# Keys' norm per token and head: root and reciprocal on a 128x10 tile, spread back over the channels by TensorE

## The chip, the cores and the metric

The kernel runs on one core of one Trainium2 chip. The metric is the device time of one launch in microseconds, the lower the better.

## The reference

Two layers of a trunk for 128 prompt tokens and 512 latent tokens (640 together, five tiles of 128). The even layer mixes tokens with a bidirectional RWKV-7 scan over 12 heads of 64 channels. The part that the change touches is the normalised key of each token and head, which enters the scan twice, as `kk` and as `kk * a`:

```python
kf = k.astype(f32)
kk = heads(kf * k_k)
kk = kk / jnp.maximum(jnp.linalg.norm(kk, axis=-1, keepdims=True), 1e-12)
...
s_kk = jnp.einsum('zbhvk,zbhk->zbhv', S, kk_t)
S = (S * w_t[..., None, :] - s_kk[..., None] * (kk_t * a_t)[..., None, :]
     + v_t[..., :, None] * k_t[..., None, :])
```

After the scan come a group norm, a bonus term and a gate, then the output projection, and after each mixer an expert-choice mixture of 16 SwiGLU experts. The odd layer has a convolution and a chunked gating in place of the scan. All arithmetic is in 32-bit floats.

## The kernel before, in words

The twelve heads are handled as six head pairs: a pair's 2 x 64 channels lie on the 128 partitions and its 640 tokens on the free axis. `even_heads` does all six. It first builds the features of pair 0 (called the opening below), then runs `heads(True)` five times and `heads(False)` once. Each engine runs its own queue in the order written, and the engines meet only in named semaphores.

A turn of `heads(True)` scans pair i and, in the gaps that the scan leaves, builds the features of pair i+1. Its first part masks the products of queries and keys (VectorE, L1574) and inverts them (the many 64x64 matmuls L1014 to L1060 and L1582). Its second part is a chain of four steps j = 0 to 3 that passes the state from tile to tile. A step goes through: `old_state(j)` on TensorE (L952, L955), a copy on ScalarE, a matmul (L1103), a copy on ScalarE, a pair of matmuls (L1115, L1116), and `advance(j)` on VectorE (L1600, L1603), which lets `old_state(j+1)` go. Between these links TensorE takes pieces for the next pair from the table `FILL` by `ahead(n)`, with n = 3j, 3j+1 and 3j+2: the projections of queries (Q) and values (VV), chunk by chunk (L893), and `knorm`. Its third part sums the outputs y (L1125 to L1134), multiplies the gate (L1140) and takes the mean over a head (L1144); then the next turn begins with L972.

The norm is made as follows. ScalarE squares the scaled key into `kk`, a 128x640 tile (`k_squares`). `knorm` multiplies it by `headones`, a 128x128 matrix with ones where both channels are of the same head, so that every channel gets its head's sum (L909). ScalarE takes the root of the 128x640 result (`k_root`, L1233), and VectorE in `normed_k` the maximum with 1e-12 (L1435), the reciprocal (L1437) and the product with the key (L1439). `norm_features` (L1469, L1471) and `key_queries` (L1486) read the result.

`shift(s)` (L1422, L1424) blends each token of Q, K or VV with its neighbours. Before it ScalarE copies the projection (`copy_raw`, L1194) and GpSimd adds the neighbours (L1368). `copy_raw(VV)` also waits for `r_shifted`, which `shift(Q)` gives. `bonus_input` (L1476) gives `ahead_done`, on which ScalarE's copy of y waits (L1321); after that copy TensorE can take the mean (L1144).

In the opening, TensorE's order is: projection of K, low ranks, `knorm(2)`, projection of Q, a slab of the modulation weights (`slabs`, L463), projection of VV, three slabs, and `mod_turn` (L474), which waits for ScalarE's `copy_rows`. VectorE's order is: `shift(K)`, both decays, both `key_features` (the last of them L1462 and L1463), `normed_k`, `norm_features`, `shift(Q)`, queries, `shift(VV)`, `bonus_input`, then `take_mods` (L491), which waits for `mod_turn`, and then the masks L1574. Only after `take_mods` may TensorE do its second group of L972 (`ymean_read`).

Of the kernel before, what the change touches and what calls it, by code (L numbers as in the profile page):

```python
# [17 lines left out]
ALU = mybir.AluOpType  # L18
# [7 lines left out]
P = 128  # L26
# [4 lines left out]
NT = T // P  # L31
# [38 lines left out]
def build(nc, t):  # L70
    ctx = ExitStack()
    with ctx:
# [42 lines left out]
        def pair(q):  # L115
            return psf[:, q * 1024:q * 1024 + T]
# [650 lines left out]
        def even_heads():  # L767
# [30 lines left out]
            ecc = ca(2, NT)  # L798
            proj, shf, rkv, kk = x[:, 0:2], x[:, 2:4], x[:, 4:7], x[:, 7]
# [27 lines left out]
            with stage() as block:  # L827
# [54 lines left out]
                def _(pe):  # L882
# [22 lines left out]
                    def knorm(q):  # L905

                        pe.wait_ge(sem("sq_ready"), 1).then_inc(sem("sq_ready"), -1)
                        for a, b in halves:
                            last = pe.matmul(pair(q)[:, a:b], headones, kk[:, a:b], start=True, stop=True)  # L909
                        last.then_inc(sem("e_ready"), 1)  # L910

# [7 lines left out]
                    def take_weights():  # L919
# [9 lines left out]
                        6: (lambda: slot_read(2), lambda: project(VV, 0, (0, 1))),  # L929
# [3 lines left out]
                        10: (lambda: project(VV, 0, (7,)),),  # L933
# [235 lines left out]
                    slot_read()  # L1169
                    project(Q, 0, range(KC))  # L1170
# [4 lines left out]
                    slot_read(3)  # L1175
                    mod_turn(pe, PARTS - EARLY, 5)
# [5 lines left out]
                def _(act):  # L1182
# [47 lines left out]
                    def k_root(q):  # L1230

                        act.wait_ge(sem("e_ready"), 1).then_inc(sem("e_ready"), -1)
                        act.activation(kk, pair(q), ACT.Sqrt).then_inc(act_done, 1)  # L1233
                        done("e_read", "knorm_root")
# [149 lines left out]
                def _(dve):  # L1384
# [47 lines left out]
                    def normed_k():  # L1432

                        dve.wait_ge(sem("knorm_root"), 1).then_inc(sem("knorm_root"), -1)
                        dve.tensor_scalar(kk, kk, 1e-12, None, ALU.max).then_inc(dve_done, 1)  # L1435
                        done()
                        dve.reciprocal(kk, kk).then_inc(dve_done, 1)  # L1437
                        done()
                        dve.scalar_tensor_tensor(kk, rkv[:, K], col("k_k"), kk, ALU.mult, ALU.mult).then_inc(dve_done, 1)  # L1439
                        done()  # L1440

# [125 lines left out]
                    def heads(i, following):  # L1567
# [56 lines left out]
                        if following:  # L1624
                            key_features(1)
                            normed_k()
                        advance(2)
                        if following:
                            norm_features(0)
                            norm_features(1)  # L1630
                            shift(Q)
# [22 lines left out]
                    normed_k()  # L1654
# [1151 lines left out]
```

## Time and profile before

| what | us |
|---|---|
| median of 3 runs (2413.72, 2414.37, 2420.5) | 2414.37 |
| span of the profiled execution | 2406.1 |
| the six reciprocals of 128x640 (L1437), first and last start | 174.5, 753.1 |

The profiled execution has no whole time of its own on record, only its span from first to last instruction; the median of the runs lies 8.3 us above it. TensorE is busy 94% of the span (2250.6 us), VectorE 40%, ScalarE 16%, GpSimd 7%. The even layer's heads fill 152 to about 860 us; most of the remainder are the two expert mixtures, in which the DMA row of the page stands at 9, that is 90% or more. A share of busy time says little here, because within a turn the engines hand work to each other: the views in order of time, engine by engine, are the ones to read.

### The profile page before, as it was taken

How to read it: one execution, taken by the hardware profiler on the slowest of the kernel's cores; microseconds unless marked ns; L12 is line 12 of the kernel's file. 1: busy time of each engine (PE TensorE's matmuls, PEld its weight loads, DVE VectorE, ACT ScalarE, POOL GpSimd, SP SyncE). 2: the span in 40 equal slices, each digit the busy share in tenths (PEclk: the TensorE clock that was granted, in tenths of full speed). 3: DMA queues.
4: the chain of work that ended last, by engine and by line, in shares of the span. 5: the costliest groups of instructions: out<-in, count | busy, mean ns of one | idle time of the engine just before them, and what ended most of it. 6: DMA issues, size and time to landing. Idle time of an engine off the chain costs nothing. (4 is left out here: it accounts for less than half of the span.)

```text
span 2406.1 us, 55266 instructions
## 1 busy us (share of the span) xinstructions
PE 2250.6 (94%) x23172; PEld 1269.3 (53%) x23172; DVE 965.6 (40%) x1785; ACT 396.9 (16%) x685; POOL 166.7 (7%) x162
## 2 busy tenths in 40 slices
PE   5998998989899789999999999889998999999997
PEld 2446776767676665544444444545555444444444
DVE  2357767676777621311111111479613111111113
ACT  2022323232323201100000000211312000000001
POOL 1001010000011000000000000000000000000000
PEclk8998999999999999999999999899999999999999
DMA  9971010101010026699999999602036999999995
GB/s 370 391 308 32 3 33 3 33 3 34 4 33 21 3 69 244 247 379 396 396 392 397 392 395 392 211 1 70 1 140 246 396 397 395 392 397 392 392 391 173
DMA packets 181703, 539.12 MB, mean 224 GB/s; under 512 B 12545, under 2 KB 54145, under 8 KB 181410
## 3 DMA queue, kind: packets, MB, share of 16 engines
q1 hardware_dynamic: 175202, 515.16, 55.6%
q0 software_dynamic: 6336, 21.63, 3.8%
q8 instruction: 119, 1.95, 0.3%
q14 instruction: 46, 0.38, 0.0%
HBM read 510.81 MB, written 25.95 MB: 223 GB/s over the span
## 5 line engine op out<-in xcount | busy, mean ns | idle before, releaser
L2045 PE MATMUL ps<-raw,xs 128*64 128x512 f32 x3072 | 670.9, 594 | 4.2 <-PEq L2039 4.2
L2045 PEld LDWEIGHTS ps<-raw,xs 128*64 128x64 f32 x3072 | 217.3, 137 | 428.6 <-issue 427.2
L2057 PE MATMUL ps<-raw,xs 128*32 128x256 f32 x6144 | 342.5, 380 | 2.3 <-PEq L2039 2.2
L2057 PEld LDWEIGHTS ps<-raw,xs 128*32 128x32 f32 x6144 | 195.2, 110 | 133.2 <-issue 9.9
L2236 DVE SCALAR_TENSOR_TENSOR h<-h,ps 128x768 f32<-128x768 f32 x32 | 30.5, 953 | 461.2 <-DVEq L2235 461.2
L893 PE MATMUL ps<-h,wk 128*128 128x512 f32 (+1 forms) x576 | 175.3, 444 | 1.5 <-PEq L1160 1.3
L1582 DVE COPY_PREDICATED wk<-m,ps 128x512 f32<-128x512 uint8 x180 | 130.7, 732 | 98.7 <-DVEq L1581 97.7
L893 PEld LDWEIGHTS ps<-h,wk 128*128 128x128 f32 x576 | 93.3, 190 | 76.2 <-issue 73.6
L2363 PE MATMUL ps<-h,raw 128*128 128x512 f32 (+1 forms) x448 | 124.7, 440 | 7.2 <-PEq L2354 7.2
L2164 ACT ACTIVATE h<-ps 128x768 f32<-128x768 f32 x32 | 26.0, 811 | 591.8 <-ACTq L2163 591.8
L1020 PE MATMUL ps<-wk 64*64 64x64 f32 x2400 | 107.3, 224 | 10.2 <-issue 7.0
L1026 PE MATMUL ps<-wk 64*64 64x64 f32 x2160 | 100.3, 222 | 3.8 <-issue 3.8
L1039 PE MATMUL ps<-wk 64*64 64x64 f32 x2400 | 99.0, 218 | 4.9 <-issue 4.7
L2363 PEld LDWEIGHTS ps<-h,raw 128*128 128x128 f32 x448 | 69.0, 193 | 62.4 <-issue 62.4
L1277 ACT ACTIVATE wk<-ps 128x256 f32<-128x256 f32 (+1 forms) x180 | 65.7, 366 | 191.2 <-ACTq L1276 191.0
L2624 DVE SCALAR_TENSOR_TENSOR wk<-wk 128x670 f32<-128x670 f32 x116 | 96.3, 905 | 0.4 <-DVEq L2618 0.4
L2020 POOL DMA_INDIRECT ysum<-rows,idx x30 | 43.1, 1438 | 752.4 <-POOLq L2018 743.5
L1020 PEld LDWEIGHTS ps<-wk 64*64 64x64 f32 x2400 | 86.1, 133 | 15.2 <-issue 10.6
L1039 PEld LDWEIGHTS ps<-wk 64*64 64x64 f32 x2400 | 86.7, 135 | 4.9 <-issue 4.8
L2225 DVE TENSOR_TENSOR xs<-ps,mod 128x512 f32<-128x512 f32 x68 | 30.2, 486 | 141.5 <-DVEq L2222 141.5
L1026 PEld LDWEIGHTS ps<-wk 64*64 64x64 f32 x2160 | 82.2, 134 | 6.4 <-issue 6.2
L1574 DVE TENSOR_TENSOR wk<-ps,tables 128x512 f32<-128x512 f32 x120 | 74.5, 683 | 15.6 <-DVEq L1573 15.6
(331 smaller groups left out, 2558.8 us busy)
## 6 DMA issues: line engine op xcount, KB each, us to landing
raw<-in_moe_w_gate SPq DMA_DIRECT2D x64, 2048.0 KB, 17.2
raw<-in_moe_w_up SPq DMA_DIRECT2D x64, 2048.0 KB, 17.4
raw<-in_moe_w_down SPq DMA_DIRECT2D x64, 2048.0 KB, 18.0
wk<-in_mod_w SPq DMA_DIRECT2D x24, 2048.0 KB, 10.6
wk<-in_ev_w_in SPq DMA_DIRECT2D x18, 512.0 KB, 5.3
raw<-in_od_w_in SPq DMA_DIRECT2D x4, 2048.0 KB, 18.0
hrow<-rows SPq DMA_DIRECT2D x10, 512.0 KB, 3.2
ysum<-low SPq DMA_DIRECT2D x10, 512.0 KB, 8.8
```

What stands on the lines that cost most here:

```text
L893: last = pe.matmul(pair(q)[:, a:b], win[:, c, s], h[:, c, a:b], start=c == 0, stop=c == KC - 1)
L1020: pe.matmul(ps[lo:hi, zb, slotT(z, hh):slotT(z, hh) + HD], yw[lo:hi, g, z, hh], invT(g, z, hh, lo, hi), start=True, stop=True)
L1026: last = pe.matmul(ps[to:te, zb + 1, slotN(z, hh):slotN(z, hh) + HD], lhs, rhs, start=True, stop=True)
L1039: last = pe.matmul(ps[to:te, 2 + u % 2, at:at + HD], mat[lo:hi, g, z, hh, 0, lo:hi], inv(g, z, hh, lo, hi), start=True, stop=True)
L1277: act.activation(yw[:, g].rearrange("p z h n -> p (z h n)")[:, 0:w], ps[:, 2 + u % 2, 0:w], ACT.Copy).then_inc(sem("yw_copied"), 1)
L1574: dve.tensor_tensor(mat[:, tt, z, hh].rearrange("p k n -> p (k n)"), ps[:, 4 + (n + 2) % 4], tri[:, z], ALU.mult).then_inc(sem("mat_read"), 1)
L1582: dve.copy_predicated(xx[:, g].rearrange("p z k h n -> p z k (h n)"), bcast(lv[:, q // NT], 2, 2), ps[:, zbank(q):zbank(q) + 2, 0:4 * HD]. ...
L2020: pool.indirect_dma_start(t["ysum"][:, :], bass.IndirectOffsetOnAxis(idx[:, e:e + 1], 0), ys[:, ee], None, compute_op=ALU.add).then_inc(se ...
L2045: last = pe.matmul(ps[to:to + CAPS, bank_of(kind, ee)], XS[ee][:, c, 0:CAPS], raw[:, slot(l, 2 * m + c // 4), c % 4, 8 * to:8 * to + 512], ...
L2057: last = pe.matmul(ps[to:to + 32, bank_of(kind, ee) + 1, 0:256], XS[ee][:, c, CAPS:], raw[:, slot(l, 2 * m + c // 4), c % 4, 8 * to:8 * to ...
L2363: last = pe.matmul(place(q)[:, a:b], win[m // 4][:, c, m % 4 * P:(m % 4 + 1) * P], h[:, c, a:b], start=c == 0, stop=c == KC - 1)
L2624: dve.scalar_tensor_tensor(to, src, cw[:, c, k:k + 1], to, ALU.mult, ALU.add).then_inc(sem("tap"), 1)
```

## The change

`knorm` now takes each tile of 128 tokens of the squares as the stationary operand and two columns of `headones` as the moving one, so that the sums stand with the tokens on the partitions: 128 x (5 tiles x 2 heads). Root, maximum and reciprocal run on that tile, `krate`. `spread_krate` sends it back over the channels: for each tile and head a matmul with the rate, broadcast over 64 columns, as stationary operand and the identity as moving one. `normed_k` then multiplies the key by the result in PSUM. On TensorE `spread_krate` stands, in a turn, after the first two chunks of VV (`ahead(6)`), and in the opening between `knorm(2)` and the projection of Q. On VectorE, in a turn, `shift(Q)` moves from behind `norm_features` to between `k_rate` and `normed_k`; in the opening it stays where it was. In the opening and in `ahead(10)` TensorE waits once more, for `krate_read`.

```diff
--- before.py
+++ after.py
@@ -796,6 +796,7 @@
             sout = ca(2, HD)
             stmp = ca(2, P)
             ecc = ca(2, NT)
+            krate = ca(NT, 2)
             proj, shf, rkv, kk = x[:, 0:2], x[:, 2:4], x[:, 4:7], x[:, 7]
             lw = (lw0, kk)
             icl = (proj[:, 0], shf[:, 0])
@@ -905,9 +906,21 @@
                     def knorm(q):
 
                         pe.wait_ge(sem("sq_ready"), 1).then_inc(sem("sq_ready"), -1)
-                        for a, b in halves:
-                            last = pe.matmul(pair(q)[:, a:b], headones, kk[:, a:b], start=True, stop=True)
+                        for tt in range(NT):
+                            last = pe.matmul(pair(q)[:, 2 * tt:2 * tt + 2], kk[:, tt * P:(tt + 1) * P], headones[:, 0::HD], start=True, stop=True)
                         last.then_inc(sem("e_ready"), 1)
+
+                    def krate_read():
+
+                        pe.wait_ge(sem("krate_read"), 1).then_inc(sem("krate_read"), -1)
+
+                    def spread_krate(q):
+
+                        pe.wait_ge(sem("krate_ready"), 1).then_inc(sem("krate_ready"), -1)
+                        for tt in range(NT):
+                            for hh, (lo, hi) in enumerate(HALF):
+                                last = pe.matmul(pair(q)[lo:hi, tt * P:(tt + 1) * P], bcast(krate[:, tt, hh], 1, HD), ident, start=True, stop=True)
+                        last.then_inc(sem("krate_spread"), 1)
 
                     def bonus():
 
@@ -926,11 +939,11 @@
                         3: (lambda: slot_read(), lambda: project(Q, 0, (0, 1, 2))),
                         4: (lambda: project(Q, 0, (3, 4, 5)),),
                         5: (lambda: slot_read(), lambda: knorm(1), lambda: project(Q, 0, (6, 7))),
-                        6: (lambda: slot_read(2), lambda: project(VV, 0, (0, 1))),
+                        6: (lambda: slot_read(2), lambda: project(VV, 0, (0, 1)), lambda: spread_krate(1)),
                         7: (lambda: project(VV, 0, (2, 3)),),
                         8: (lambda: project(VV, 0, (4, 5)),),
                         9: (lambda: project(VV, 0, (6,)),),
-                        10: (lambda: project(VV, 0, (7,)),),
+                        10: (lambda: project(VV, 0, (7,)), lambda: krate_read()),
                     }
 
                     def ahead(n):
@@ -1167,12 +1180,14 @@
                     slot_read()
                     knorm(2)
                     slot_read()
+                    spread_krate(2)
                     project(Q, 0, range(KC))
                     slabs(20, 21)
                     slot_read()
                     project(VV, 1, range(KC))
                     slabs(21, 2 * PARTS)
                     slot_read(3)
+                    krate_read()
                     mod_turn(pe, PARTS - EARLY, 5)
                     for i in range(HP - 1):
                         heads(True)
@@ -1230,7 +1245,7 @@
                     def k_root(q):
 
                         act.wait_ge(sem("e_ready"), 1).then_inc(sem("e_ready"), -1)
-                        act.activation(kk, pair(q), ACT.Sqrt).then_inc(act_done, 1)
+                        act.activation(krate, pair(q)[:, 0:2 * NT].rearrange("p (t h) -> p t h", h=2), ACT.Sqrt).then_inc(act_done, 1)
                         done("e_read", "knorm_root")
 
                     def copy_r(j, bank):
@@ -1429,15 +1444,21 @@
                         if s == Q:
                             dve.sem_inc(sem("r_shifted"), 1)
 
-                    def normed_k():
+                    def k_rate():
 
                         dve.wait_ge(sem("knorm_root"), 1).then_inc(sem("knorm_root"), -1)
-                        dve.tensor_scalar(kk, kk, 1e-12, None, ALU.max).then_inc(dve_done, 1)
+                        dve.tensor_scalar(krate, krate, 1e-12, None, ALU.max).then_inc(dve_done, 1)
                         done()
-                        dve.reciprocal(kk, kk).then_inc(dve_done, 1)
+                        dve.reciprocal(krate, krate).then_inc(dve_done, 1)
                         done()
-                        dve.scalar_tensor_tensor(kk, rkv[:, K], col("k_k"), kk, ALU.mult, ALU.mult).then_inc(dve_done, 1)
+                        dve.sem_inc(sem("krate_ready"), 1)
+
+                    def normed_k(q):
+
+                        dve.wait_ge(sem("krate_spread"), 1).then_inc(sem("krate_spread"), -1)
+                        dve.scalar_tensor_tensor(kk, rkv[:, K], col("k_k"), pair(q), ALU.mult, ALU.mult).then_inc(dve_done, 1)
                         done()
+                        dve.sem_inc(sem("krate_read"), 1)
 
                     inc, exc = slice(1, P + 1), slice(0, P)
                     fb = (eN[:, 0, :, inc], eP[:, 1, :, exc])
@@ -1623,12 +1644,13 @@
                         advance(1)
                         if following:
                             key_features(1)
-                            normed_k()
+                            k_rate()
+                            shift(Q)
+                            normed_k(1)
                         advance(2)
                         if following:
                             norm_features(0)
                             norm_features(1)
-                            shift(Q)
                             key_queries(True)
                             shift(VV)
                             bonus_input()
@@ -1651,7 +1673,8 @@
                     decay(1, (lw0, bon))
                     key_features(0)
                     key_features(1)
-                    normed_k()
+                    k_rate()
+                    normed_k(2)
                     norm_features(0)
                     norm_features(1)
                     shift(Q)
```

## Rows read from the trace of the kernel before

A row of a view in order of time has: start us, us, engine, line, operation, out<-in, form, how many records; in brackets the idle time before it and what ended it. "Q" behind an engine is its sequencer. A 32-bit matmul of one tile leaves two records. Windows have: us, busy us (records), granted clock, and the DMA's share and GB/s.

**Rows 1.** The page: its head and the engines' busy time.

```profile
span 2406.1 us, 55266 instructions
...
PE 2250.6 (94%) x23172; PEld 1269.3 (53%) x23172; DVE 965.6 (40%) x1785; ACT 396.9 (16%) x685; POOL 166.7 (7%) x162
```

**Rows 2.** Groups by line and form, 140 to 860 us: busy us, mean ns.

```profile
L1512 DVE RECIPROCAL x<-x 128x160 f32<-128x160 f32 x24 | 27.2, 1132 | 0.0
...
L1437 DVE RECIPROCAL x<-x 128x640 f32<-128x640 f32 x6 | 24.9, 4152 | 0.9
```

**Rows 3.** Order of time, VectorE, before the first head pair: start, us, idle before.

```profile
171.81 1.72 DVE L1462 TENSOR_TENSOR wk<-wk 128x640 f32<-128x640 f32 x1 [0.26 <-DVEq L1461]
173.45 0.16 DVE L1463 COPY wk<-wk 128x5 f32<-128x5 f32 x1
173.87 0.49 DVE L1435 TENSOR_SCALAR x<-x 128x640 f32<-128x640 f32 x1 [0.26 <-DVEq L1434]
...
196.44 0.90 DVE L491 TENSOR_TENSOR mod<-ps,vec 128x16 f32<-128x16 f32 x10 [0.44 <-DVEq L486]
...
198.67 2.48 DVE L1574 TENSOR_TENSOR wk<-ps,tables 128x512 f32<-128x512 f32 x4 [0.26 <-DVEq L1573]
...
204.39 2.48 DVE L1574 TENSOR_TENSOR wk<-ps,tables 128x512 f32<-128x512 f32 x4 [2.20 <-DVEq L1573]
```

**Rows 4.** Order of time, TensorE, before the first head pair.

```profile
161.65 8.82 PE L893 MATMUL ps<-h,wk 128*128 128x512 f32 x32
...
181.10 5.36 PE L463 MATMUL ps<-wk 128*32 128x512 f32 x48
...
188.29 2.24 PE L474 MATMUL ps<-tables,mix 128*128 128x20 f32 x16 [1.83 <-PEq L472]
...
197.63 2.08 PE L972 MATMUL ps<-wk 64*128 64x256 f32 x8 [5.09 <-PEq L966]
```

**Rows 5.** Windows of 1 us: length, TensorE busy, granted clock, DMA share, GB/s.

```profile
1607.00:1608.00 1.00, 0.00 (x0) 1.00 0.00 0
...
1611.00:1612.00 1.00, 0.35 (x1) 0.50 0.00 0
...
1616.00:1617.00 1.00, 1.00 (x3) 0.74 0.00 0
```

**Rows 6.** Order of time, TensorE, end of the first turn of heads.

```profile
282.29 1.25 PE L909 MATMUL ps<-x,cst 128*128 128x512 f32 x4
...
287.03 2.40 PE L893 MATMUL ps<-h,wk 128*128 128x512 f32 x8
...
289.27 1.00 PE L1103 MATMUL ps<-wk 128*128 128x64 f32 x8
...
292.33 0.39 PE L1115 MATMUL ps<-wk 128*128 128x128 f32 x2
...
296.45 0.46 PE L952 MATMUL ps<-wk 128*128 128x128 f32 x2 [0.90 <-PEq L950]
...
301.46 0.66 PE L1130 MATMUL ps<-wk 128*64 128x128 f32 x8
...
301.95 0.39 PE L1134 MATMUL ps<-wk 128*64 128x128 f32 x4
...
310.36 1.32 PE L1144 MATMUL ps<-x,cst 128*128 128x512 f32 x4 [0.95 <-PEq L1142]
```

**Rows 7.** Order of time, VectorE, the same stretch.

```profile
288.85 0.53 DVE L1435 TENSOR_SCALAR x<-x 128x640 f32<-128x640 f32 x1 [0.26 <-DVEq L1434]
...
294.96 0.42 DVE L1600 TENSOR_TENSOR wk<-ps,wk 128x256 f32<-128x256 f32 x1 [0.26 <-DVEq L1597]
...
300.40 0.82 DVE L1422 SCALAR_TENSOR_TENSOR x<-x 128x640 f32<-128x640 f32 x1 [0.26 <-DVEq L1421]
...
306.04 0.82 DVE L1422 SCALAR_TENSOR_TENSOR x<-x 128x640 f32<-128x640 f32 x1 [1.85 <-DVEq L1421]
```

**Rows 8.** Order of time, ScalarE, the same stretch.

```profile
302.54 0.70 ACT L1194 ACTIVATE x<-ps 128x640 f32<-128x640 f32 x1 [2.08 <-ACTq L1193]
...
309.39 0.70 ACT L1321 ACTIVATE x<-ps 128x640 f32<-128x640 f32 x1 [6.14 <-ACTq L1320]
```

## Prediction, made before the changed kernel ran

> **What bounds the kernel now.** I read the page first for where vector work is dense, then the groups by form for the price of what goes, then the views in order of time, one engine at a time, in the opening and in one turn of heads. The span is 2406.1 us and TensorE is busy 94% of it [rows 1], so what VectorE saves counts only where TensorE waits for VectorE. The six reciprocals take 24.9 us in all [rows 2], the upper bound for what their going can give. The runs' median is 8.3 us above the span; I form differences inside the profiled execution and add their sum to the median.
>
> The opening has two chains side by side. VectorE's runs without a real pause from the key features over the norm at 173.87 to `take_mods` at 196.44 and the first masks at 198.67 [rows 3]. TensorE's runs ahead of it: projection of Q from 161.65, one slab, VV, three slabs until 181.10 + 5.36 = 186.46, `mod_turn` from 188.29 to 190.53, and then it waits 5.09 us until 197.63 [rows 4]. So VectorE sets the end and TensorE has slack: its last `mod_turn` record ends at 190.53, VectorE takes the result at 196.44, which with 0.3 us for the hop leaves 5.6 us.
>
> In a turn the two alternate. VectorE reaches `advance(2)` at 294.96 [rows 7], yet the matmuls it waits for began at 292.33 and, four records of each of two lines at 0.22 us a pair, were done at about 293.4 [rows 6]: VectorE is late by 1.5 us. TensorE notices 0.90 of it at 296.45 and nothing until 310.36 [rows 6]. There it waits 0.95 us for ScalarE's copy of y at 309.39 [rows 8], which in turn waited for `bonus_input`, the end of VectorE's chain from `shift(Q)` at 300.40 over `copy_raw(VV)` at 302.54 to `shift(VV)` at 306.04 [rows 7, 8].
>
> **The change part by part.** Removed from VectorE, six times: the 128x640 maximum (0.53 [rows 7]) and the reciprocal (4.15 [rows 2]). Added: the same on ten columns. From 1132 ns for 160 columns and 4152 for 640 [rows 2] a column costs 6.3 ns and the start 0.13 us, so ten cost 0.19 us; the maximum is like the five-column L1463, 0.16 us [rows 3]. With completions that is 0.67 us in place of 4.95. ScalarE's root gets shorter too, which nobody waits for.
>
> `knorm`: before, four records in 283.37 - 282.29 = 1.08 us. After, ten records with a full stationary tile and two moving columns. The nearest are L1103, eight records of 64 columns from 289.27 to the next piece at 290.11, 0.105 each [rows 6], and L474 with 20 columns, 16 in 2.24 us, 0.14 each [rows 4]. So 1.05 to 1.4; I take 1.05, no change. The Trainium skill says in "TensorE: Matmul & The Clock Gate", section "Wait — 56ns, not 53.3ns?", that start to start never falls below about 25 ns however few the columns; ten records would be 0.25 us by it, an estimate. The rows at 0.105 and 0.14 are well above that floor, and the sum would be the same by either, because in both places the spread behind it waits for VectorE.
>
> `spread_krate`: ten matmuls with 64 stationary and 128 moving columns, in alternating halves. L1130 has that form: eight records in 301.95 - 301.46 = 0.49 us [rows 6], so 20 records take 1.22 us. Were each matmul to run alone at some 0.285 us, it would be 2.85; below, nothing is free of cost under L1130's pitch but the idle time that it may fill, so 0 is the lower end. I take 1.22, since the row is of the very form.
>
> *The opening.* TensorE's queue now holds `spread_krate(2)` ahead of the projection of Q, and it waits for `k_rate`, which on VectorE comes after both key features. That point was at 173.87. The L1462 before it took 1.72 us beside GpSimd's addition for Q; that addition now falls later, and L1422 with as many columns takes 0.82 alone [rows 7], so 0.9 comes off: 172.97. Add 0.67 and a hop of 0.1: TensorE goes on at 173.75. The spread takes 1.22, so Q starts at 175.0 and not at 161.65 [rows 4]: 13.3 us later. Behind it in the same queue stand everything to `mod_turn` and the first L972.
>
> The stop is 12 us long. After the pause that covers 1607 the granted clock was 0.50 when work resumed at 1611.65, and full again only at 1616.5 [rows 5], 4.9 us of work at 1.2 GHz in place of 2.4, of which half is lost: 2.5 us. I take the same here. TensorE's chain is then 15.8 us late, and `mod_turn` ends at 206.3. VectorE can take it at 206.6 in place of 196.44: +10.2. VectorE's own chain arrives about then: the VV projection ends at 181.10 + 15.8 = 196.9, then 3.5 us for copy and neighbours (302.54 to 306.04 [rows 7, 8]), 3.2 for shift and bonus input (306.04 to what let 309.39 go), and up to 2.1 if GpSimd's other work runs beside it: 205.9. All that VectorE saved here lies idle. Given back: in the profile shown TensorE came out of its 5.09 us wait at the lower clock and made VectorE wait 2.20 us at 204.39 [rows 3, 4]; that pause disappears, so I return 0.9, somewhat under half of it. The opening ends 9.3 us later.
>
> *Each of five turns.* `k_rate` begins where L1435 did, 288.85 [rows 7], and releases TensorE at about 289.75. TensorE finishes its two VV chunks at 289.27 [rows 6] and waits 0.5. The spread ends at 291.0, so L1103 is 1.7 us later and, nothing idle in between, L1115 too: at 294.05. Its products are ready at 295.1, against VectorE's 294.96 before: the 1.5 us by which VectorE was late are used up, and `advance(2)` starts 0.3 later. Now TensorE is the late one: `old_state(3)` starts at 297.25, 0.8 later. Behind it TensorE waits for nothing up to the gate that follows y, so y, done at about 308.15 before, is done at 308.95. The other branch to ScalarE's copy at 309.39 gets shorter: `shift(Q)` is done before, so `copy_raw(VV)` waits only for its own projection, 302.1 (its end at 301.25 in the trace, plus the 0.85) in place of 302.54, and VectorE has `bonus_input` done by 308.8. The copy starts at 309.2 in place of 309.39, 0.2 us earlier. Five turns give -1.0 us. With the spread at 2.85 a turn is 1.4 longer (y at 310.55), with it at 0 some 0.8 shorter: -4 to +7 us over five. The added `krate_read` waits are for something long done. Nothing queued behind VectorE's new wait `krate_spread` is late: `advance(2)` waits for TensorE beyond it. The last turn builds no pair and is unchanged.
>
> Sum: 9.3 - 1.0 = +8.3, and 2414.4 + 8.3 = 2422.7 us. What follows the heads (output projection, mixture weights) starts from their end and moves with it.
>
> **The rivals.** First, the stop costs no clock: then TensorE is 13.3 late, `take_mods` +7.7, less 1.8 since then more of the 2.20 us pause is given back, the opening +5.9, the whole +4.9, 2419.3 us. For it: the 2.5 us pause before `knorm` brought no slow records behind it (Q's 32 in 8.82 [rows 4]). Against: rows 5, with a pause of 7 us, and this one is 12. I give this case 0.27. The Trainium skill, in "TensorE: Matmul & The Clock Gate", section "What's actually happening", has the throttled clock as the default that activity lifts; by it this case would have no chance, and the sum would stay at +8.3.
>
> Second, the turns pay: the spread runs at its serial price, or the 0.5 us waits and later products let the clock fall once more in some turns. Five times 1.4 on 9.3 is +16, 2430.7 us. Against: L1130's pitch. 0.11.
>
> Third, faster: VectorE's chain sets both places and the stop in the opening is taken up by slack. Then the opening gains about 3 us (4.95 + 0.9 less 0.67, a spread of 1.5 and its hop), and each turn the full 1.5 us that `advance(2)` was late: -3 - 7.5 = -10.5, 2403.9 us. It decides from the point where TensorE's queue has more slack than the 13.3 us; the trace shows 5.6. That leaves 0.05.
>
> That the change doesn't do what it says would be a reciprocal with a large fixed price; the two rows give 0.13 us, so I give it nothing.
>
> **How the numbers follow.** My forecast has 0.57. A difference under 0.3%, 7.2 us, can't be told from none. The forecast's own spread is about 3 us for the unknown clock phase, so some 0.36 of its 0.57 lies over 7.2, and of the first rival a fifth, 0.06. With the second that is 0.53; but a projection started later also shifts the clock dips of every turn, either way, which I let lift slower to 0.56, same 0.38, faster 0.06. The range reaches from the first rival less its turns' lower bound, about 2416.5, to 2428.5, between forecast and second rival.
>
> **What would show it.** TensorE idle for about 12 us before the projection of Q in the opening, then about 5 us at the 0.50 clock; the first L1574 at about 209 and not at 198.67; L1437 at 0.2 us; in the turns L1103 some 1.7 us after the end of the VV chunks, VectorE waiting for it before `advance(2)`, and the distance between the same instructions of two turns within 0.3 us of before. Wrong it would be if Q starts before 172, if the first masks come less than 7 us later, or if a turn changes by more than 1 us.

## The result, and the profile after

The changed kernel took 2432.0 us (median of 4 runs, 2428.3 to 2435.5) against 2416.7 us (2413.7 to 2420.5): a ratio of 1.0065, 95% interval 1.0050 to 1.0079. The medians differ by 15.3 us, and the ratio times the median of before is 15.7 (12.1 to 19.1); all differences in time below are formed in this second way. Timed again three times it gave 1.0049 (1.0030 to 1.0068), 1.0044 (1.0029 to 1.0059) and 1.0042 (1.0028 to 1.0055). The plain mean of the four ratios is 1.0050: the change costs about 12 us. I had forecast +8.3 us, 2422.7 us and a range up to 2428.5 us: the direction and the place were right, the size too small.

The head of the page after, to stand beside [rows 1]:

```profile
span 2430.2 us, 55608 instructions
...
PE 2264.8 (93%) x23328; PEld 1282.1 (53%) x23328; DVE 935.8 (39%) x1785; ACT 395.0 (16%) x685; POOL 164.1 (7%) x162
```

VectorE is busy 29.8 us less, more than the six reciprocals of [rows 2] held, and the span is 24.1 us longer. This span is not the measure of the change: a second and a third trace of the kernel before have 2410.6 and 2421.0 us, so the one shown ahead was a short one. The new reciprocal, by line and form (busy us, mean ns, idle before):

```profile
L1452 DVE RECIPROCAL wk<-wk 128x10 f32<-128x10 f32 x6 | 1.3, 217 | 0.9
```

The opening, VectorE in order of time, against [rows 3]:

```profile
175.59 0.17 DVE L1450 TENSOR_SCALAR wk<-wk 128x10 f32<-128x10 f32 x1 [0.26 <-DVEq L1449]
...
178.97 0.88 DVE L1459 SCALAR_TENSOR_TENSOR x<-x,wk,ps 128x640 f32<-128x640 f32 x1 [2.85 <-DVEq L1458]
...
192.50 0.82 DVE L1437 SCALAR_TENSOR_TENSOR x<-x 128x640 f32<-128x640 f32 x1 [8.64 <-DVEq L1436]
...
208.75 0.91 DVE L491 TENSOR_TENSOR mod<-ps,vec 128x16 f32<-128x16 f32 x10 [2.62 <-DVEq L486]
...
210.99 2.48 DVE L1595 TENSOR_TENSOR wk<-ps,tables 128x512 f32<-128x512 f32 x4 [0.26 <-DVEq L1594]
...
215.32 2.48 DVE L1595 TENSOR_TENSOR wk<-ps,tables 128x512 f32<-128x512 f32 x4 [0.81 <-DVEq L1594]
```

The first K copy of this trace is 2.6 us later than in the one before, for reasons ahead of the change; less that, `take_mods` (L491) is 9.7 us later than at 196.44, and the second set of masks (215.32) 8.3 us later than at 204.39. VectorE, which had no pause to speak of, now waits 2.85 us for the spread (ahead of L1459) and 8.64 us for Q (ahead of L1437). TensorE in the same stretch, against [rows 4]:

```profile
163.21 1.25 PE L910 MATMUL ps<-cst,x 128*128 128x2 f32 x10 [1.72 <-PEq L908]
...
176.42 2.40 PE L922 MATMUL ps<-cst,wk 128*64 128x128 f32 x20 [11.97 <-PEq L919]
...
178.75 10.55 PE L894 MATMUL ps<-h,wk 128*128 128x512 f32 x32
...
206.67 1.93 PE L474 MATMUL ps<-tables,mix 128*128 128x20 f32 x16 [1.37 <-PEq L472]
```

One row carries the result: 11.97 us of waiting ahead of the spread (L922). The projection of Q, 8.82 us long in [rows 4], takes 10.55, and the spread 2.40. Windows of 1 us, with TensorE's records alone, say why (length, TensorE busy, granted clock, DMA share, GB/s):

```profile
165.00:166.00 1.00, 0.00 (x0) 0.51 0.89 311
...
176.00:177.00 1.00, 0.58 (x6) 0.50 0.00 0
...
182.00:183.00 1.00, 1.00 (x5) 0.95 0.00 0
```

The granted clock has fallen to 0.51, the lower of its two levels (1.2 GHz), some 0.6 us after the last `knorm` record at 164.46, and is back at 182.1, 5.7 us after work resumed. What those 5.7 us did would have taken half of them at the upper level: 2.8 us lost, against the 2.5 that I took from [rows 5]. What made it fall is taken up with the experiments; it was not the stop.

One turn of heads, TensorE and VectorE in order of time, against [rows 6, 7]:

```profile
294.17 1.18 PE L910 MATMUL ps<-cst,x 128*128 128x2 f32 x10
...
298.78 2.40 PE L894 MATMUL ps<-h,wk 128*128 128x512 f32 x8
...
301.61 1.31 PE L922 MATMUL ps<-cst,wk 128*64 128x128 f32 x20 [0.42 <-PEq L919]
...
302.85 1.10 PE L1116 MATMUL ps<-wk 128*128 128x64 f32 x8
...
306.01 0.39 PE L1128 MATMUL ps<-wk 128*128 128x128 f32 x2
...
309.06 0.39 PE L965 MATMUL ps<-wk 128*128 128x128 f32 x2
...
321.78 1.31 PE L1157 MATMUL ps<-x,cst 128*128 128x512 f32 x4
```

```profile
294.49 0.43 DVE L1621 TENSOR_TENSOR wk<-ps,wk 128x256 f32<-128x256 f32 x1 [1.17 <-DVEq L1618]
...
300.73 0.22 DVE L1450 TENSOR_SCALAR wk<-wk 128x10 f32<-128x10 f32 x1 [0.26 <-DVEq L1449]
...
307.21 0.42 DVE L1621 TENSOR_TENSOR wk<-ps,wk 128x256 f32<-128x256 f32 x1 [2.45 <-DVEq L1618]
...
316.84 0.82 DVE L1437 SCALAR_TENSOR_TENSOR x<-x 128x640 f32<-128x640 f32 x1 [2.62 <-DVEq L1436]
```

And ScalarE, against [rows 8]:

```profile
313.84 0.70 ACT L1209 ACTIVATE x<-ps 128x640 f32<-128x640 f32 x1 [0.84 <-ACTq L1208]
...
320.80 0.71 ACT L1336 ACTIVATE x<-ps 128x640 f32<-128x640 f32 x1 [6.26 <-ACTq L1335]
```

Count from `advance(1)`, at 294.49 here and 11.89 us earlier in the kernel before:

```profile
282.60 0.42 DVE L1600 TENSOR_TENSOR wk<-ps,wk 128x256 f32<-128x256 f32 x1 [1.17 <-DVEq L1597]
```

L1116 (was L1103) is 1.7 us later than at 289.27, `advance(2)` at 307.21 is 0.4 later than at 294.96, `old_state(3)` at 309.06 is 0.7 later than at 296.45, and yet the copy of y at 320.80 is 0.5 earlier than at 309.39, because `copy_raw(VV)` at 313.84, 0.6 earlier, no longer waits for `shift(Q)`. VectorE, late by 1.5 us before, now waits 2.45 us ahead of `advance(2)`. Here the reader sees the whole exchange: VectorE was given 4.3 us and TensorE's queue got 1.24 us more to do (301.61 to 302.85), and at these links VectorE now waits for TensorE (2.45 us), while `old_state(3)` and the mean (L1157) have no wait ahead of them.

**How the traces are summed below.** From each trace I take the opening (first L1194 to the first L1512 of the turns; lines of the kernel before), the turns (from there to the last L1530, starts of the records in each case) and the rest (from there to the first L402 at the program's end). From the view of waits I add TensorE's waits named "issue" between 205 and 895 us, and from windows of 1 us the time that TensorE lost at the lower clock in the turns (busy time x (1 - clock)).

| trace | opening | turns | issue | clock | rest |
|---|---|---|---|---|---|
| before | 70.6 | 668.4 | 17.0 | 7.8 | 1505.1 |
| before, 2nd | 70.7 | 671.3 | 16.9 | 11.2 | 1505.1 |
| before, 3rd | 70.6 | 673.5 | 17.6 | 14.6 | 1512.2 |
| changed | 79.0 | 675.0 | 23.4 | 8.5 | 1511.6 |
| changed, 2nd | 79.0 | 676.8 | 19.0 | 14.3 | 1514.7 |
| changed, 3rd | 79.1 | 677.1 | 24.1 | 10.8 | 1513.3 |
| changed, 4th | 79.0 | 674.7 | 22.8 | 6.7 | 1509.2 |
| opening alone | 79.0 | 673.3 | 19.2 | 8.2 | 1506.6 |
| opening alone, 2nd | 78.9 | 676.7 | 19.1 | 8.1 | 1502.0 |
| turns alone | 70.8 | 669.8 | 19.3 | 6.5 | 1515.7 |
| opening, late spread, and turns | 65.6 | 676.1 | 23.1 | 11.7 | 1507.6 |

The opening repeats to 0.1 us between traces of one program. The rest does not: it differs by 7 us between three traces of the kernel before. On the mean of four traces against three, the changed kernel is longer by 8.4 us in the opening, 4.8 in the turns and 4.7 in the rest, though nothing was changed in the rest. The spans of these traces differ by 18.2 us on the mean, where the times differ by 12: the executions that were traced happened to be long ones of the changed kernel and short ones of the kernel before. So of the table only the opening can be set against a time; a difference of 5 us in the turns or in the rest can be chance.

### The profile page after: what moved, and what is told of

Same layout as the page of the kernel before. It is cut to its first block and busy times, and to the rows that moved or that the text cites. A ratio compares the mean times of both kernels' runs of the same rounds, so it can differ in the third digit from the quotient of the medians.

```text
span 2430.2 us, 55608 instructions
## 1 busy us (share of the span) xinstructions
PE 2264.8 (93%) x23328; PEld 1282.1 (53%) x23328; DVE 935.8 (39%) x1785; ACT 395.0 (16%) x685; POOL 164.1 (7%) x162
## 5 line engine op out<-in xcount | busy, mean ns | idle before, releaser
L1033 PE MATMUL ps<-wk 64*64 64x64 f32 x2400 | 108.6, 225 | 6.9 <-issue 3.6
L1052 PE MATMUL ps<-wk 64*64 64x64 f32 x2400 | 101.9, 220 | 8.7 <-issue 8.5
L1039 PE MATMUL ps<-wk 64*64 64x64 f32 x2160 | 102.5, 223 | 6.3 <-issue 6.3
L1033 PEld LDWEIGHTS ps<-wk 64*64 64x64 f32 x2400 | 86.9, 134 | 17.1 <-issue 12.1
L1595 DVE TENSOR_TENSOR wk<-ps,tables 128x512 f32<-128x512 f32 x120 | 74.5, 684 | 13.9 <-DVEq L1594 13.9
```

Source lines behind the costliest of these rows:

```text
L1033: pe.matmul(ps[lo:hi, zb, slotT(z, hh):slotT(z, hh) + HD], yw[lo:hi, g, z, hh], invT(g, z, hh, lo, hi), start=True, stop=True)
L1039: last = pe.matmul(ps[to:te, zb + 1, slotN(z, hh):slotN(z, hh) + HD], lhs, rhs, start=True, stop=True)
L1052: last = pe.matmul(ps[to:te, 2 + u % 2, at:at + HD], mat[lo:hi, g, z, hh, 0, lo:hi], inv(g, z, hh, lo, hi), start=True, stop=True)
L1595: dve.tensor_tensor(mat[:, tt, z, hh].rearrange("p k n -> p (k n)"), ps[:, 4 + (n + 2) % 4], tri[:, z], ALU.mult).then_inc(sem("mat_read"), 1)
```

## The experiments

**Control.** The kernel before, unchanged.

> The kernel before once more, unchanged, for a second trace of it and for the spread of its executions. Both theories: within 0.1% of itself. Its trace should show the same start of the heads (first K copy at 151.9 us) and the same turn lengths within 1 us; if instead the stretches of the inversions wander by 1 us a turn and the time before the heads by 2 to 3 us here too, such differences between one trace of before and one of after say nothing of the change.

Ratio 1.0005 (0.9994 to 1.0017). The first K copy came at 153.3 us and the turns were 2.9 us longer than in the first trace of the same program. So a difference of 3 us between two single traces of the turns says nothing of a change, and the +6.6 us of the first trace after could not be read as an effect.

**The change cut in two.** The new norm in the opening alone, and in the turns alone:

```diff
 # opening alone: the turns (q == 1) keep the old form
-                        for tt in range(NT):
-                            last = pe.matmul(pair(q)[:, 2 * tt:2 * tt + 2], kk[:, tt * P:(tt + 1) * P], headones[:, 0::HD], start=True, stop=True)
+                        if q == 1:
+                            for a, b in halves:
+                                last = pe.matmul(pair(q)[:, a:b], headones, kk[:, a:b], start=True, stop=True)
+                        else:
+                            for tt in range(NT):
+                                last = pe.matmul(pair(q)[:, 2 * tt:2 * tt + 2], kk[:, tt * P:(tt + 1) * P], headones[:, 0::HD], start=True, stop=True)
...
-                            k_rate()
-                            shift(Q)
-                            normed_k(1)
+                            normed_k_old()
...
+                            shift(Q)
```

> The new norm in the opening alone (the first head pair); the five turns keep the old norm, its place, and shift(Q) behind norm_features. Theory A, the stop of TensorE in the opening is the price of the change: +8 to +12 us against the kernel before, most of the 15 us of the whole change. Theory B, the five turns pay about half of it: +8 us here and the rest elsewhere. In the trace the first masks come 8 us later than before, counted from the first copy of K, and the turns have their old form.

> The new norm in the five turns alone; the opening keeps the old one. Theory A: -2 to +2 us against the kernel before. Theory B: +5 to +8 us, by 1 to 1.6 us a turn. If the two halves add up, this and the run with the opening alone sum to about 15 us.

The opening alone: 1.0057 (1.0042 to 1.0072), +13.8 us, and repeated 1.0048 (1.0032 to 1.0063), +11.6 us. The turns alone: 0.9997 (0.9988 to 1.0007), -0.7 us. The price is the opening's; theory B falls as it was put, and the forecast of -1.0 us for the turns stands. The opening alone costs 3 to 5 us more than the 8.4 by which its traces show it longer. Its turns, whose instructions are those of before, are 675.0 us on the mean of two traces against 671.1, so the excess needs no change in the turns.

**One line moved.** `spread_krate(2)` behind the projection of Q and a slab:

```diff
-                    spread_krate(2)
                     project(Q, 0, range(KC))
                     slabs(20, 21)
+                    spread_krate(2)
```

> The changed kernel with the opening's spread moved in TensorE's queue from ahead of the projection of Q to behind that projection and one slab; nothing else. TensorE should reach it at about 172.5 and wait 1.3 us in place of 12. Both theories: the opening's 8.3 us go, so 8 to 10 us less than the changed kernel. Theory A: +0 to +5 us against the kernel before, the same as the turns alone; theory B: +5 to +8. The opening itself could be up to 3 us shorter than before, as VectorE has 4.3 us less to do there.

1.0010 (0.9998 to 1.0023) against before: the 12 us are gone. TensorE in its opening waits for nothing at the spread:

```profile
162.87 10.58 PE L894 MATMUL ps<-h,wk 128*128 128x512 f32 x32
...
175.23 1.31 PE L922 MATMUL ps<-cst,wk 128*64 128x128 f32 x20
```

VectorE's chain now sets the end of the opening again. L1497 takes 3.03 us beside a copy by GpSimd (L1390, 190.98, 2.32 us); the kernel before has a record of 2.96 us beside the same copy (L1422, 190.95):

```profile
190.95 3.03 DVE L1497 SCALAR_TENSOR_TENSOR x<-x,wk 128x640 f32<-128x640 f32 x1 [0.16 <-DVEq L1402]
...
194.42 0.91 DVE L491 TENSOR_TENSOR mod<-ps,vec 128x16 f32<-128x16 f32 x10 [0.44 <-DVEq L486]
```

The opening is 65.6 us, 13.4 shorter than the changed kernel's and 5.0 shorter than before. Nothing of the 5.0 shows in the time; its turns have 23.1 us of issue waits, on which more below.

The same trace shows where the lower clock came from. The projection of Q, right behind `knorm` and without a stop, takes 10.58 us and not 8.82, and the windows read:

```profile
163.00:164.00 1.00, 1.00 (x4) 0.85 1.07 438
...
165.00:166.00 1.00, 1.00 (x2) 0.50 1.01 393
...
167.00:168.00 1.00, 1.00 (x5) 0.95 0.92 373
```

The clock fell although TensorE worked on. It does so 0.5 to 0.9 us after `knorm` in each of the eleven traces that have the new `knorm` in the opening, and there in none of the seven with the old one, although TensorE's pause ahead of it is 1.7 to 2.6 us in all of them (2.49 us here and in the kernel before). So what brings the fall is the new form, ten small matmuls behind that pause in place of four of 128x512, and the stop only keeps the clock low: for 17 us in the changed kernel, and from 163.7 to 167.0 here, where the lost 1.8 us are hidden behind VectorE.

**The stop filled.** Matmuls with an unused result while TensorE waits, first 33, then 16:

```diff
+                    for _ in range(33):
+                        pe.matmul(ps[:, 3, P:512], ident, h[:, 0, 0:384], start=True, stop=True)
                     spread_krate(2)
```

> The changed kernel with 33 extra matmuls (128x384, result unused) on TensorE in the opening, ahead of its wait for the rates, about 11 us of work in the 12 us stop. Nothing else. If the lower clock after the stop is part of the price (theory A: 2.5 to 2.9 us of it), the granted clock stays at 1.00, the spread takes 1.3 us and not 2.4, the projection of Q 8.8 and not 10.5, and the kernel is 2 to 3 us faster than the changed one. If the clock costs nothing at the end, the time stays.

The filler was priced wrong: 33 took not 11 but 23.2 us (66 records),

```profile
162.85 23.23 PE L1184 MATMUL ps<-h,cst 128*128 128x384 f32 x66
```

so the opening grew to 88.6 us and the kernel to 1.0065 (1.0050 to 1.0079). This run doesn't answer its question. It shows, though, that 18.0 us more in the opening cost 15.7 us (12.1 to 19.1) at the end.

> The changed kernel with 16 filler matmuls in the stop of the opening; the 33 of the earlier run took 23.2 us, so these take 11.3 and end inside the 12 us wait. The granted clock should stay at 1.00 through the spread and the projection of Q: opening 76.0 us in place of 79.0, and the kernel about 3 us faster than the changed one. If its time is the same as the changed one's, the opening's end does not pass on to the end one to one.

```profile
164.02 12.26 PE L1184 MATMUL ps<-h,cst 128*128 128x384 f32 x32
...
176.24 1.31 PE L922 MATMUL ps<-cst,wk 128*64 128x128 f32 x20
...
177.48 8.92 PE L894 MATMUL ps<-h,wk 128*128 128x512 f32 x32
```

Spread and projection run at full clock (1.31 and 8.92 us), the opening is 76.0 us, and the ratio 1.0033 (1.0016 to 1.0049), +8.0 us, with the unfilled kernel at +11.8 on the same chip. The clock did not stay at 1.00, as I had expected: it fell all the same, to 0.50 in the windows from 165 to 168 us, but now the unused matmuls bore it. So the lower clock cost the changed opening 3.0 us: shown in the trace, and of the expected size in the time (3.8), whose intervals overlap.

**Pads.** Small matmuls in the kernel before, where TensorE has slack in the opening (`n` is 13, then 28):

```diff
                     slot_read(3)
+                    for _ in range(n):
+                        pe.matmul(ps[:, 3, P:P + HD], ident, ident[:, 0:HD], start=True, stop=True)
```

> The kernel before with 13 small matmuls (26 records, as many as the change adds to the opening) where TensorE has 5.6 us of slack in the opening: their 2 to 3 us are hidden. Theory C, the extra instructions move the points at which TensorE's queue stalls for its next instructions (about every 120 matmul records in the heads) relative to the work: the time in issue stalls between 200 and 900 us moves away from the 16.4 us of both traces of the kernel before, and the kernel is 0 to 4 us slower. Against it (theory A): stalls as before, time within 1 us.

> The same with 28 small matmuls (56 records). Theory C: issue stalls differ from both the kernel before and the run with 13, by some us either way, and the time follows. Theory A: time within 1 us of before, as 4 to 6 us of filler still fit the slack within 1 us.

Opening 70.7 and 70.8 us, as before: the pads are hidden. But the issue waits in the turns, whose instructions are the same, are 15.4 us with 13 pads and 22.4 with 28. The times are 0.9994 (0.9984 to 1.0005) and 1.0005 (0.9997 to 1.0014): the order agrees with theory C, the intervals overlap. That instructions added in one place change the stalls in another is seen in the traces. Their price is not one to one: with 28 pads the issue waits are 5.2 us above the mean of the kernel before, and the time +1.2 us, at most +3.4.

**shift(Q) moved alone.** The move on VectorE that the change makes in the turns, without the new norm:

```diff
                             key_features(1)
+                            shift(Q)
                             normed_k()
                         advance(2)
...
-                            shift(Q)
```

> The kernel before with shift(Q) moved ahead of normed_k in the five turns, norm unchanged: copy_raw(VV) no longer waits for it, but advance(2) comes 2 us later on VectorE. If VectorE sets advance(2) (294.96 against products at 293.4, my prediction's reading), old_state(3) comes 2 us later and the turn is 1 to 2 us longer: +5 to +9 us in all. If the branch over copy_raw(VV) sets the turn, it is 0.4 us shorter a turn: -2 us.

1.0070 (1.0055 to 1.0085), +16.9 us. VectorE and TensorE in its second turn:

```profile
414.75 0.82 DVE L1422 SCALAR_TENSOR_TENSOR x<-x 128x640 f32<-128x640 f32 x1 [0.73 <-DVEq L1421]
...
423.05 0.43 DVE L1600 TENSOR_TENSOR wk<-ps,wk 128x256 f32<-128x256 f32 x1 [0.26 <-DVEq L1597]
```

```profile
417.78 0.39 PE L1115 MATMUL ps<-wk 128*128 128x128 f32 x2
...
424.54 0.46 PE L952 MATMUL ps<-wk 128*128 128x128 f32 x2 [3.53 <-PEq L950]
...
427.79 1.80 PE L1103 MATMUL ps<-wk 128*128 128x64 f32 x8
```

The matmuls for `advance(2)` begin at 417.78, VectorE reaches it at 423.05, and `old_state(3)` waits 3.53 us, where it waited 0.90. That VectorE set this link is shown, and so is what the cheap reciprocal buys in the turns: room for a move that by itself costs 3.4 us a turn. I had expected 1 to 2, and the waits are about that. The rest is clock: behind the longer wait L1103 takes 1.80 us in place of 1.00, and this trace loses 20.1 us to the lower clock in its turns, where the kernel before loses 7.8 to 14.6. Of its turns' 690.5 us, 19.4 more than the mean of before, about 9 are clock and 1.5 issue waits, which leaves 1.8 us a turn.

**More traces and times of the same programs.**

> The changed kernel once more, unchanged: a second trace and more timings. Theory D, by now: the time of the heads is a fixed part of about 644 us (between the first reciprocal of the first turn and the last gate product) plus what the lower clock and the issue stalls take, and these two wander from execution to execution; then this trace has another sum of stalls than 22.5 us. Theory C: the stalls belong to the program, and it has 22 to 23 us again. The opening is 79.0 us (first K copy to that reciprocal) in both; the time +12 to +18 us against before.

> The changed kernel, third trace. Theory D: first K copy, turns and rest scatter around those of the kernel before, opening 79.0 us; the time +8 to +12 us once enough executions are in. The other theory: first K copy at 154.5 us or later again, time +12 us or more.

> The kernel before, third trace. Theory D: its first K copy may be as late as 154.5 us too, its turns 668 to 676 us, its rest 1505 to 1515. The other theory: first K copy at 151.9 to 153.6 us. Time within 2 us of itself.

> The new norm in the opening alone, second trace and timing. Theory D: +8 to +10 us. The other theory: +12 us or more, with the first K copy at 154.5 us or later.

> The changed kernel, fourth trace, as the run before it: both theories as there.

The other theory was that the changed kernel starts its heads later. Nothing of it is left: the changed kernel's third trace has the first K copy at 151.5 us, and the third of before at 154.3. Theory D, that stalls and clock wander from execution to execution, is half right. What each turn loses to the clock does wander (6.7 to 14.6 us in the seven). The issue waits wander less than they differ between programs: 16.9 to 17.6 us in three traces of the kernel before, 19.0 to 24.1, mean 22.3, in four of the changed one. The view of waits, TensorE, 205 to 895 us, first trace of the changed kernel and third trace of before (engine, line, waited for: us in total, times, longest):

```profile
PE ps L1052 <- issue: 8.5, 9, 2.0
...
PE ps L1039 <- issue: 6.3, 5, 2.0
...
PE ps L1033 <- issue: 3.6, 8, 1.2
...
PE ps L1073 <- issue: 3.2, 2, 1.6
```

```profile
PE ps L1020 <- issue: 7.8, 8, 1.9
...
PE ps L1039 <- issue: 5.5, 7, 1.2
...
PE ps L1050 <- issue: 2.5, 3, 1.1
...
PE ps L1026 <- issue: 1.8, 3, 1.4
```

And they stand mostly at the same instructions in each execution of a program. Two of them in the changed kernel, then the same two in its third trace, whose clock reads some 3 us less:

```profile
268.72 0.21 PE L1052 MATMUL ps<-wk 64*64 64x64 f32 x1 [1.28 <-issue]
...
504.00 0.73 PE L1063 MATMUL ps<-wk 64*64 64x64 f32 x10 [1.82 <-issue]
```

```profile
265.90 0.21 PE L1052 MATMUL ps<-wk 64*64 64x64 f32 x1 [1.02 <-issue]
...
500.51 0.97 PE L1063 MATMUL ps<-wk 64*64 64x64 f32 x10 [1.55 <-issue]
```

Neighbouring such waits in a dense stretch are 122 to 126 matmul records apart, in all traces. Taking "issue" and clock out, the turns are 643.6, 643.2 and 641.3 us in the three traces of before and 643.1, 643.5, 642.2 and 645.2 in the four of the changed kernel: means of 642.7 and 643.5. So the norm itself costs the turns nothing that can be seen, while the changed program's turns are 4.8 us longer (means 675.9 and 671.1): 5.2 more in issue waits, 1.1 less in clock, 0.8 other. This remainder is no constant of the kernel, though: in the two traces of the opening alone, with the old turns, it is 645.9 and 649.5 us, and there the issue waits are only 2.0 above before.

The Trainium skill, in "Runtime: NRT & Kernel Launch", has instructions of 64 bytes ("What's in a NEFF") and an instruction memory that is refilled in blocks of 16 KiB ("Terms"). That is 256 instructions; 125 matmul records with as many weight loads, and a few waits, are about that, and by the profile's part on queues (packets, MB, share) the queue of kind "instruction" moved 16.4 KB a packet:

```profile
q8 instruction: 119, 1.95, 0.3%
```

So the trace agrees with the rule in the spacing, and it shows that the waits are refills: by the DMA records of that queue, each of the 408 issue waits between 205 and 895 us in the eighteen traces ends 2.1 to 2.9 us after one of these packets starts. The packets are about 8 us apart on the mean (85 to 88 in 690 us), and of TensorE's 1262 waits with another cause 6% end at such a distance.

**Candidates.** The late spread in the opening with the turns as before, and the late spread with a changed turn:

```diff
 # turns of the second candidate
-                        6: (..., lambda: project(VV, 0, (0, 1)), lambda: spread_krate(1)),
+                        6: (..., lambda: project(VV, 0, (0, 1))),
-                        8: (lambda: project(VV, 0, (4, 5)),),
+                        8: (lambda: spread_krate(1), lambda: project(VV, 0, (4, 5))),
...
                             shift(Q)
-                            normed_k(1)
                         advance(2)
                         if following:
+                            normed_k(1)
```

> The new norm in the opening alone, with the spread behind the projection of Q and one slab; the five turns as before. The opening is 65.6 us in place of 70.6, as in the run with both, and nothing is added in the turns: -5 us against before if the opening passes on in full; 0 if, as in the run with both (+2.4 at a -5 us opening), something takes it back.

> A candidate: the opening with the late spread, and in the turns spread_krate(1) behind the matmuls that advance(2) waits for, with normed_k(1) behind advance(2) on VectorE. L1103 is 1.7 us earlier again, advance(2) 1.4 us earlier than in the kernel before, old_state(3) about where it was; each turn 0.3 to 0.7 us shorter than before. With the opening 5 us shorter: -5 to -8 us against before.

0.9992 (0.9979 to 1.0004), -1.9 us, and 0.9995 (0.9979 to 1.0012), -1.2 us: neither is told apart from the kernel before. Their openings are 67.4 and 65.7 us; in the second the issue waits are 21.3 us, 4.1 above before, which would take back most of its 4.9. The first speaks against such a sum: its opening is 3.2 us shorter and its issue waits, 13.9 us, 3.3 less, and yet its time is only 1.9 us less (5.1 at most). No version was found that surely beats the kernel before.

## Why the prediction was wrong

**Right, step by step.** The turns: -1.0 us forecast, -0.7 (-2.9 to +1.7) with the change in the turns alone. The stop: 12.1 us forecast, 11.97 in the trace. Its reason, the spread's place ahead of the projection of Q in TensorE's queue: moving the one line removed the cost. The clock: 2.5 us forecast, 2.8 by the windows, 3.0 by the filled run; the size was right and the reason was not, since the clock falls behind the new `knorm` without any stop. `take_mods` +10.2 forecast, +9.7 measured; the opening +9.3 forecast, +8.4 in six traces; of the pause ahead of the second masks 1.4 us were given back (196.44 and 204.39 before, 208.75 and 215.32 after) and not 0.9. VectorE's own chain was ready 2.4 us before the 205.9 forecast, which cost nothing, as it then waited 2.62 us for `mod_turn`. `knorm` 1.05 forecast, 1.04 measured (294.17 to 295.21); the spread 1.22 and 1.24; `k_rate` about as forecast, its reciprocal 217 ns for 190. In the turn, L1103 +1.7 forecast and measured, `advance(2)` +0.3 and +0.4, `old_state(3)` +0.8 and +0.7, the copy of y -0.2 and -0.5.

**The step that failed** is the sum, "9.3 - 1.0 = +8.3", with "What follows the heads [...] starts from their end and moves with it": everything behind the opening, but for the part of a turn that the change touches, was put at no change because its instructions are the same. The runs show in its place that the opening alone, 8.4 us longer, costs 13.8 and 11.6 us at the end. So this term was sized at 9.3 and measured 12.7 on the mean; the turns' term was right. The other 4 us arise behind the opening. In the traces both the turns (+4.8 us; +3.9 with the opening alone) and the rest (+4.7) are longer, but neither by more than it differs between traces of one kernel. A wait that I had not read is part of it: "issue", 17.0 us in the turns already in the profile before, and 22.3 on the mean in the changed kernel. Its places hang on how many instructions went ahead, and the change adds 26 matmul records to the opening and to each turn.

**What was chance.** The first timing lay high and the base low. The base of the forecast, 2414.4 us, was the median of three runs, and a fourth brought it to 2416.7: 2.3 of the 9.3 us between 2422.7 and 2432.0. The later ratios 1.0049, 1.0044 and 1.0042 on 2414.4 would give 2426.2, 2425.0 and 2424.5 us, all below 2428.5. That the first timing came out above the range is thus in part bad luck. The 4 us that the sum lacks are clear on the mean of the six timings of the change and of the opening alone (12.3 us), not in each: the intervals of the three later timings of the change reach down to 7 us.

**The rivals.** That the stop costs no clock: refuted, and its argument too. It said that the 2.5 us pause before `knorm` brought no slow records behind it; with the new `knorm` the same pause did (10.58 us for Q with the late spread). That the turns pay: its +16 us are near the first timing, and that is luck, since the turns alone cost nothing and the spread took 0.124 us a matmul and not 0.285. That VectorE sets both places: in the opening refuted, in the turn true of the kernel before (shown by the move of `shift(Q)`) and gone after.

**What stays open.** The stop, the lower clock and the 8.4 us of the opening are shown, with their causes. The 5 us of further issue waits in the changed program's traces are measured, and that they are refills is shown. That they are the missing 4 us in its time is not shown. For it: 8.4 and 5.2 make 13.6, and the four timings have a mean of 12. Against it: the opening alone, with only 2.0 more of them, costs as much as the whole change; the turns alone have 19.3 us and cost nothing; and 28 pads have 22.4 us and cost 1.2. Nor is the excess a fixed sum: with 33 fillers the opening was 18.0 us longer and the time 15.7. Timings of one program differ by up to 5.6 us from one time to the next, which is as much as what is looked for. Separating it would need a change of instruction count with no other effect and many more executions.

## What to carry to other kernels

Before moving a producer to a faster form, find its consumer in the other engine's queue and read what stands behind it: here a wait of 12 us put ahead of an 8.8 us projection cost 8.4 us where the reciprocal had freed 4.3, and one line's move gave it back. Work taken from one engine and given to another wins at most what the receiving engine waited at that link; read that wait first (0.90 us here) and compare it with the added work (1.24 us). Read the "issue" waits of a dense stretch too: they change when instructions are added ahead (15.4, 17.2 and 22.4 us with 13, no and 28 pads). And before a time is explained by single traces, look at whether the traced executions are typical: here they added 6 us to the difference.

## What the runs showed that I had not expected

A 128x384 matmul in 32-bit floats from a 128x128 stationary tile took 0.65 us at the upper clock (33 took 11.0 us more than 16), where I had put 0.33. Ten small matmuls in place of four wide ones brought the granted clock down behind them, with a stop or without; with the stop it was still at 0.50 for 5.7 us of the work after it. TensorE's waits without a releaser were refills of its instructions, up to 2.0 us each. And moving 2 us of VectorE work ahead of one link of the chain cost 3.4 us a turn, about half of it through the clock.
